# Loading the attention branch back earlier, into staging tiles of its own

## The reference

```
y_att = (o_att * silu(az)) @ w_br_att          # softmax attention, 8 heads
o_dn  = rms_norm(bidir_gated_deltanet(...))     # 8 heads, two directions, chunks of 128 tokens
y_dn  = (o_dn * silu(dz)) @ w_br_dn
mix   = (sigmoid(gate_att) * y_att + sigmoid(gate_dn) * y_dn) @ w_out
```

## Time and profile before

| | |
|---|---|
| time before, median of three (us) | 2302.9 |
| lowest, highest (us) | 2298.47, 2304.11 |
| profiled execution (us) | 2299.77 |
| its span (us) | 2298.0 |
| TensorE matmul busy | 2200.8 us, 96% |
| VectorE, ScalarE, GpSimd busy | 52%, 44%, 11% |
| mean granted TensorE clock | 0.987 |

### The profile page before, as it was taken

One profiled execution on the slowest core, in us unless ns is written; L12 is line 12 of the kernel. 1 busy time (PEld: TensorE's weight loads), 2 busy tenths in 40 slices (PEclk: granted clock), 3 DMA queues, 4 the chain that ended last, 5 costly groups with the idle time before them and its releaser, 6 DMA issues.

```text
span 2298.0 us, 35314 instructions
## 1 busy us (share of the span) xinstructions
PE 2200.8 (96%) x14886; PEld 1696.2 (74%) x14886; DVE 1189.3 (52%) x2101; ACT 1011.5 (44%) x1919; POOL 247.9 (11%) x273
## 2 busy tenths in 40 slices
PE   6999999999999999899999999999999989999999
PEld 4777776777777877686656888888876556888887
DVE  5566666666644446532335553444557665443442
ACT  4565656556554236534554331233445544331331
POOL 0022121221120011102221000001001001000000
PEclk9999999999999999999999999999999989999999
DMA  4221221221214332121111322232221112322232
GB/s 169 70 97 57 70 71 52 85 83 61 66 62 139 132 137 79 53 71 55 37 35 63 110 92 92 94 108 92 74 74 45 39 38 66 107 92 92 92 104 80
DMA packets 34766, 185.79 MB, mean 81 GB/s; under 512 B 4000, under 2 KB 4384, under 8 KB 15408
## 3 DMA queue, kind: packets, MB, share of 16 engines
q1 hardware_dynamic: 34608, 183.53, 23.6%
HBM read 172.99 MB, written 7.90 MB: 79 GB/s over the span
## 4 chain that ended last, share of the span: by engine, by line
PE 86%; DVE 7%; ACT 3%; issue 2%; DMA 1%; POOL 0%; SPq 0%; POOLq 0%; DVEq 0%; ACTq 0%
PE ps L1549 85%; PE ps L1552 1%; ACT arena L2439 1%; DVE spl L1989 1%; DMA on_t<-spill 0%; DMA arena<-arena 0%; DMA raw<-wstream 0%; DVE x L2316 0%; DVE arena L2139 0%; DVE x L2095 0%; ACT spl L2442 0%; ACT arena L2442 0%; ACT hh L2439 0%; DVE arena L2178 0%; DVE hl L2284 0%
## 5 line engine op out<-in xcount | busy, mean ns | idle before, releaser
L1549 PE MATMUL ps<-hh,spl 128*128 128x512 f32 x3232 | 1070.2, 405 | 28.4 <-DVE arena_r L2216 7.8
L1549 PEld LDWEIGHTS ps<-hh,spl 128*128 128x128 f32 x3232 | 606.2, 189 | 185.2 <-issue 41.5
L1549 PE MATMUL ps<-hl,spl 128*128 128x512 f32 x1552 | 629.4, 406 | 0.0
L1989 DVE TENSOR_TENSOR spl<-raw,spl 128x512 fp32r<-128x512 f32 x596 | 409.4, 713 | 171.8 <-ACT spl L2442 170.9
L1549 PE MATMUL ps<-arena_r,spl 128*128 128x512 f32 x1936 | 475.1, 401 | 9.7 <-DVE arena_r L2216 4.6
L1549 PEld LDWEIGHTS ps<-arena_r,spl 128*128 128x128 f32 x1936 | 366.3, 190 | 106.5 <-DVE arena_r L2220 6.5
L2442 ACT ACTIVATE spl<-raw 128x512 fp32r<-128x512 f32 x596 | 342.2, 618 | 142.1 <-PE ps L1549 140.9
L1549 PEld LDWEIGHTS ps<-hl,spl 128*128 128x128 f32 x1552 | 293.4, 189 | 73.9 <-issue 18.4
L1549 PE MATMUL ps<-arena 32*32 32x32 f32 (+7 forms) x5664 | 217.3, 224 | 18.7 <-DVE arena L2178 6.5
L2439 ACT ACTIVATE arena<-arena 128x512 f32<-128x512 f32 (+3 forms) x211 | 139.7, 663 | 190.7 <-DVE arena L2321 141.5
L1549 PEld LDWEIGHTS ps<-arena 32*32 32x32 f32 (+4 forms) x5664 | 126.2, 115 | 104.9 <-issue 76.6
(11 more groups left out here) (216 smaller groups left out, 1904.6 us busy)
## 6 DMA issues: line engine op xcount, KB each, us to landing
raw<-wstream SPq DMA_DIRECT2D x149, 1024.0 KB, 5.0
GS<-g_rows SPq DMA_DIRECT2D x16, 256.0 KB, 3.3
spill<-x SPq DMA_DIRECT2D x14, 256.0 KB, 2.1
arena<-spill SPq DMA_DIRECT2D x12, 256.0 KB, 5.0
arena<-arena SPq DMA_DIRECT2D x20, 128.0 KB, 2.6
on_t<-spill SPq DMA_DIRECT2D x10, 256.0 KB, 2.9
x<-xT SPq DMA_DIRECT2D x4, 512.0 KB, 6.7
spill<-arena SPq DMA_DIRECT2D x8, 256.0 KB, 2.0
```

Of the source, the lines that this page charges most:

```text
L1549: return pe.matmul(out, lhsT, rhs, start=start, stop=stop, skip_group_check=True)
L1989: tt(spl[:, p % 2, 1, c], raw[:, p % 2, c], spl[:, p % 2, 0, c].bitcast(F32), ALU.subtract) \
```

## The change

The attention branch's eight tiles get staging tiles of their own, `A(26)`, `A(35)` and `A(36)`, of which none is used by the last head's scan or output norm. The planner's load lane no longer waits for the last head's `on_b`, but for its last inverse step `lv_q2` and for the `on_b` of the head before. The delta-rule branch's tiles keep the old staging tiles and still wait for the last `on_b`. The waits are split accordingly: each `ya` load waits for its own spill, the first `re_hi` for the end of the seventh head's scan (28 steps of `sc_o` for seven heads) and for the last `lv_q2`, the first `yd` load for all spills of `spill2`, and the first `yd` low half for all eight `ya` low halves, since two `yd_l` tiles are the staging tiles `A(35)` and `A(36)`.

```diff
     def load_lane():
 
-        while ("on_b", 7) not in o.at or ("at_m", 7) not in o.at:
+        while ("lv_q2", 7) not in o.at or ("on_b", 6) not in o.at:
             yield
-        o.behind(o.at["on_b", 7], o.at["at_m", 7])
+        o.behind(o.at["lv_q2", 7], o.at["on_b", 6])
         o.now += 2.0
         for which in ("ya", "yd"):
+            while which == "yd" and ("on_b", 7) not in o.at:
+                yield
+            if which == "yd":
+                o.behind(o.at["on_b", 7])
+                o.now += 2.0
             for k in range(KT):
+                while ("at_m", k) not in o.at:
+                    yield
+                if k == 7 and which == "ya":
+                    o.behind(o.at["at_m", 7])
+                    o.now += 2.0
                 while not stage_slots.ready():
                     yield
                 i, old = stage_slots.take()
...
-        stage_of = [A(26), on_t[:, 0, :], on_t[:, 1, :]]
+        stage_of = {"ya": [A(26), A(35), A(36)], "yd": [A(26), on_t[:, 0, :], on_t[:, 1, :]]}
...
                 elif q.kind == "re_ld":
                     which, k = q.key
                     if q.n == 1:
-                        for i in range(2):
-                            sp.wait_ge(sem(f"ua_out{i}"), 64)
+                        sp.wait_ge(sem("ar_out"), 10)
+                        sp.wait_ge(sem("on_b"), 7)
+                    if which == "ya":
+                        a = at["at_m", k]
+                        sp.wait_ge(sem(f"ua_out{a.i}"), 16 * a.out_n)
+                    if which == "yd" and k == 0:
                         sp.wait_ge(sem("on_out"), 128)
                     if q.old:
                         sp.wait_ge(sem("re_lo"), q.old.n)
...
                 elif kind == "re_lo":
                     which, k = q.key
+                    if which == "yd" and k == 0:
+                        w.wait_ge(sem("re_lo"), 8)
                     w.wait_ge(sem("re_hi"), q.n)
...
                 elif kind == "re_hi":
                     which, k = q.key
                     if q.n == 1:
+                        w.wait_ge(sem("sc_o"), 28)
+                        t = at["lv_q2", 7].u
+                        w.wait_ge(drained[t.b], t.n)
+                    if which == "yd" and k == 0:
                         w.wait_ge(sem("sc_o"), 32)
```

More of the change, by code:

```diff
@@ L1525, in sync @@
                     src = (spill if which == "ya" else spill2)[:, k, :]
-                    sp.dma_start(stage_of[q.i], src).then_inc(sem(f"re_ld{q.i}"), 16)
+                    sp.dma_start(stage_of[which][q.i], src).then_inc(sem(f"re_ld{q.i}"), 16)
                 elif q.kind == "load_x":
@@ L2218, in vector @@
                     which, k = q.key
+                    if which == "yd" and k == 0:
+                        w.wait_ge(sem("re_lo"), 8)
                     w.wait_ge(sem("re_hi"), q.n)
-                    tt(HI[which + "_l"][k], stage_of[q.i], HI[which + "_h"][k].bitcast(F32), ALU.subtract) \
+                    tt(HI[which + "_l"][k], stage_of[which][q.i], HI[which + "_h"][k].bitcast(F32), ALU.subtract) \
                         .then_inc(sem("re_lo"), 1)
@@ L2663, in scalar @@
                     if q.n == 1:
+                        w.wait_ge(sem("sc_o"), 28)
+                        t = at["lv_q2", 7].u
+                        w.wait_ge(drained[t.b], t.n)
+                    if which == "yd" and k == 0:
                         w.wait_ge(sem("sc_o"), 32)
                     w.wait_ge(sem(f"re_ld{q.i}"), 16 * ((q.ld.n - 1) // 3 + 1))
-                    copy(HI[which + "_h"][k], stage_of[q.i]).then_inc(sem("re_hi"), 1)
+                    copy(HI[which + "_h"][k], stage_of[which][q.i]).then_inc(sem("re_hi"), 1)
                 elif kind == "eg_sig":
```

## The result

| | before | after |
|---|---|---|
| median of six runs each (us) | 2303.35 | 2293.62 |
| lowest, highest (us) | 2298.47, 2305.66 | 2292.94, 2295.38 |
| profiled execution, its span (us) | 2299.77, 2298.0 | 2295.38, 2293.6 |
| mean granted clock | 0.987 | 0.987 |

The ratio after to before is 0.9962, 95% interval 0.995 to 0.9974. The changed kernel is 9.7 us faster by the medians, 8.8 us by the ratio (6 to 11.5 by its interval); 8.0 us was forecast, and the interval can't tell these apart.

The account below looks back on a forecast made before the run. TensorE was taken as the bound nearly everywhere, stalled at the first `ya` gemm. 7.4 + 0.7 - 0.1 = 8.0 us off gave 2291.8 from the profiled execution, 2294.9 from the median; 2294.0 was taken, range 2289.5 to 2299.5.

Parts of the forecast that it names:

- Stall: First `ya` gemm on TensorE: its waits for tiles, slow clock included, go if all eight are ready; 7.4 us saved.
- Ones' matmul: Output norm's matmul of ones, placed three matmuls later: those fill TensorE's wait on ScalarE; 0.7 us saved.
- Scan: Last head's scan: low halves moved into VectorE's gaps before `rv` may delay it; 0.1 us lost, at most 1.7.
- What is late next: After the first `ya` gemm: weight splits two and three still end before TensorE needs them, split three with 3.3 us cover.
- rival (e): SyncE's line of `yd` and weight loads: split three comes late, kernel slower, 2312.9 us if 10 us beyond 743.5; chance 0.05.
- First `ya_out`: VectorE's end of the first `ya` gemm: a sign of success if it starts at about 721.8.
- Rival (c): Later in the program: one more half-clock stretch takes back 1.7 us, gain 6.3 us, time 2296 us; chance 0.12.

Follow-up runs that it names:

- the change again: The changed kernel with nothing altered, run and profiled once more against the kernel before; median 2294.29 us, ratio 0.9968.
- the fillers: The kernel before with 25 spare matmuls put between the blocks of the first `ya` gemm; median 2301.56 us, ratio 1.0004.
- the ones later: The kernel before with only the last head's matmul of ones three matmuls later; 2304.75 us in one run, then median 2303.71 us, ratio 1.0004.

## Why the prediction was right

The forecast was 2294.0 (2289.5 to 2299.5) and 8.0 us; the time is 2293.62, and M fell by 8.0. The mechanism came as forecast. That the time was hit within 0.4 us is partly luck: 2294.0 was a choice between 2291.8 and 2294.9, the program outside M varies by more than a microsecond from run to run, and the change again had a median of 2294.29.

- **Stall, 7.4 us:** 7.3 measured. It was read as the first gemm's 13.14 us less an undisturbed gemm. The prediction said that the clock's share is in this sum; the fillers show that this share is nothing.
- **Ones' matmul, 0.7 us:** 0.65, and it stays only because the tiles no longer bound; alone it gave nothing that could be told from run to run.
- **Scan, 0.1 us:** 0.0. Both gaps held, with 0.20 and 0.06 us to spare against 0.1 forecast for each. The third load took 5.5 us against 5.39 assumed, by the one row that had the same pairing. VectorE kept 0.68 us beside `kdt`, and `kdt` grew from 1.19 to 1.75 us, hidden. The Trainium skill, page SBUF — State Buffer, section Who interferes with whom, says that a VectorE instruction with two SBUF inputs contends with a GpSimd instruction that reads SBUF, and that the issue order decides who blocks. The trace agrees that they contend. The order of the starts does not tell who pays: `kdt` started first, by 0.02 us, and was the one stretched, as the rows before had it.
- **What is late next:** VectorE ended weight split two at 727.1, TensorE's second gemm ended at 729.8; split three ended at 738.3, the fourth gemm, by two times 5.60 later, at 741.0. Cover 2.7 us each, against 2.3 and 3.3 forecast; rival (e) did not come about.
- **First `ya_out`:** forecast near 721.8; it came 33.5 us after the scan's first matmul, which is 723.0 on that scale. It stood behind a weight half and a low half of `yd` on VectorE; TensorE did not wait for it.
- **Rival (c), the clock later:** in the first profile of the change 1.0 us was lost beside a half-clock stretch that began earlier, in the second it was not. The rest of the program took as long with the ones later, which was not shifted. No run shows such a loss to be part of the change.

## What to carry to other kernels

When a consumer takes tiles one by one, look at what sets the last tile's arrival before pricing the idle time: the idle stretches and the half clock in between cost nothing here, since the arrival bound. Too few staging tiles and a large load ahead in the same queue hid each other, so that taking away either one alone looked nearly worthless. Work moved into a scan's gaps was free as long as it fitted the gap that the trace shows: 0.70 us went into 0.80 at no cost, and twice that made the first `rv` behind it 0.50 us late.

## What the runs showed of the hardware that was not expected

The same 256 KB load behind the same 1 MB load, in two profiles of one kernel, landed 7.0 and 5.7 us after its issue; in the kernel before it took 5.4. And a VectorE subtract that started 0.02 us after GpSimd's `kdt` (698.62 and 698.60) was not slowed (0.68 us), while `kdt` was: of its two instructions the first took 1.17 us in place of 0.60, the second 0.60 as before. The pair took 1.75 us again in the change again and with only half the tiles early.
